# One product for both row halves in 28 weight-stationary units of a float32 transformer forward pass

## What is computed

```
def cross_attention(h, mem_n, wq, wkv, wo):            # layers 0 and 1
    q = (h @ wq).reshape(B, S, X_HEADS, X_HEAD_DIM)
    kv = (mem_n @ wkv).reshape(B, M, 2, X_HEADS, X_HEAD_DIM)
    s = einsum('bshd,bmhd->bhsm', q, kv[:, :, 0]) * X_HEAD_DIM ** -0.5      # 1/16
    ...
def odd_mixer(h, w_in, conv_w, w_out):                 # layer 1
    proj = h @ w_in                                    # b_gate, c_gate and a third part
    z = c_gate * proj[..., 2 * CONV_DIM:]
    ...
def sq_relu_mlp(h, w1, w2):                            # all three layers, width 4096
    a = relu(h @ w1)
    return (a * a) @ w2
c_act = silu(c)                                        # layer 2: mod = c_act @ w_ada + b_ada
```

## Time and profile before

| | |
|---|---|
| median of 3 runs | 1117.59 us (1115.75 to 1118.85) |
| the profiled execution | 1117.57 us, span 1115.7 us |
| TensorE busy | 1092.0 us (98%) in 6758 products |
| VectorE busy | 701.3 us (63%) |
| ScalarE busy | 517.7 us (46%) |
| weights and other data read | 222.95 MB, 201 GB/s over the span |
| granted TensorE clock | 0.998 of full speed |

### The profile page before, as it was taken

How to read it: one execution, slowest core, us unless ns; L and a number is a source line. 1 busy time by engine, 2 the same in 40 slices (tenths; PEclk the granted TensorE clock), 3 DMA queues, 4 the chain that set the end, 5 groups by cost and what they waited for, 6 DMA issues and landing times.

```text
span 1115.7 us, 15646 instructions
## 1 busy us (share of the span) xinstructions
PE 1092.0 (98%) x6758; PEld 978.5 (88%) x6758; DVE 701.3 (63%) x666; ACT 517.7 (46%) x584; POOL 65.0 (6%) x116
## 2 busy tenths in 40 slices
PE   6999999999999999999999999999999998999998
PEld 4989899898989989998988898997888877898997
DVE  4656565487577667666546757667767477555543
ACT  5555554354444445334445453444564464453441
POOL 2200000000000000000001000001201010000000
PEclk9999999999999999999999999999999999999999
DMA  9835454446775765554545767576335373655531
GB/s 360 323 142 170 159 200 157 165 171 246 262 289 190 294 245 208 183 189 153 213 140 210 271 258 286 198 279 236 120 135 173 140 245 114 226 189 189 189 114 38
DMA packets 32356, 225.05 MB, mean 202 GB/s; under 512 B 3748, under 2 KB 4064, under 8 KB 7584
## 3 DMA queue, kind: packets, MB, share of 16 engines
q1 hardware_dynamic: 26640, 188.03, 46.8%
q0 software_dynamic: 5120, 34.85, 8.8%
q10 hardware_dynamic: 528, 1.16, 0.3%
HBM read 222.95 MB, written 1.08 MB: 201 GB/s over the span
## 4 chain that ended last, share of the span: by engine, by line
PE 92%; DVE 5%; ACT 1%; issue 1%; POOL 1%; DMA 0%; DVEq 0%; ACTq 0%; POOLq 0%
PE ps L485 46%; PE ps L470 38%; DVE lo L1540 1%; PE ps L545 1%; PE ps L723 1%; PE ps L744 1%; ACT hi L1062 1%; PE ps L898 0%; DMA h<-in_x 0%; PE ps L944 0%; DVE lo L1536 0%; DVE h L1577 0%; PE ps L877 0%; PE ps L668 0%; DVE work L1931 0%
## 5 line engine op out<-in xcount | busy, mean ns | idle before, releaser
L1540 DVE TENSOR_TENSOR lo<-raw,hi 128x2048 fp32r<-128x2048 f32 x171 | 390.9, 2289 | 180.4 <-ACT hi L1062 180.2
L1062 ACT ACTIVATE hi<-raw 128x2048 fp32r<-128x2048 f32 x171 | 326.8, 1913 | 299.4 <-PE ps L485 160.1
L470 PE MATMUL ps<-xt_hi,hi 128*128 128x256 f32 x1088 | 308.8, 284 | 0.0
L470 PE MATMUL ps<-xt_hi,lo 128*128 128x256 f32 x1088 | 307.9, 283 | 0.0
L470 PE MATMUL ps<-xt_lo,hi 128*128 128x256 f32 x1088 | 307.9, 283 | 0.0
L485 PE MATMUL ps<-hi,yt_hi 128*128 128x512 f32 x544 | 213.1, 392 | 2.8 <-DVE yt_lo L1829 1.4
L485 PE MATMUL ps<-lo,yt_hi 128*128 128x512 f32 x544 | 211.8, 389 | 0.0
L485 PE MATMUL ps<-hi,yt_lo 128*128 128x512 f32 x544 | 211.8, 389 | 0.0
L470 PEld LDWEIGHTS ps<-xt_hi,lo 128*128 128x128 f32 x1088 | 208.8, 192 | 0.8 <-issue 0.2
L470 PEld LDWEIGHTS ps<-xt_hi,hi 128*128 128x128 f32 x1088 | 208.8, 192 | 0.8 <-issue 0.2
L470 PEld LDWEIGHTS ps<-xt_lo,hi 128*128 128x128 f32 x1088 | 208.8, 192 | 0.0
(11 more groups left out here) (261 smaller groups left out, 1048.7 us busy)
## 6 DMA issues: line engine op xcount, KB each, us to landing
raw<-in_weights SPq DMA_DIRECT2D x176, 1024.0 KB, 5.0
work<-in_w_ada POOLq DMA_DIRECT2D x16, 1536.0 KB, 7.3
work<-in_gains POOLq DMA_DIRECT2D x6, 512.0 KB, 4.2
work<-mod_rows POOLq DMA_DIRECT2D x6, 512.0 KB, 7.3
h<-in_x SPq DMA_DIRECT2D x2, 512.0 KB, 6.2
work<-in_gains ACTq DMA_DIRECT2D x2, 512.0 KB, 7.1
work<-in_mem POOLq DMA_DIRECT2D x2, 512.0 KB, 9.2
work<-in_pool SPq DMA_DIRECT2D x1, 1024.0 KB, 16.1
```

The source lines that it names most:

```text
L470: mm = pe.matmul(o, ws[:, slot, k, j * P:(j + 1) * P], xs[:, c, :], start=(c == 0 and n == 0 and j % 2 == 0), stop=(c == KC - 1 and n == 2 ...
L1062: act.activation(hi[:, p % RING], raw[:, p % RING], ACT.Copy).then_inc(hi_ready, 1)
L1540: dve.tensor_tensor(lo[:, p % RING], raw[:, p % RING], hi[:, p % RING].bitcast(F32), ALU.subtract)\
```

## The change

- `unit_m` takes the place of `unit_w` in 28 units: the four query units, the first unit of each half of the convolution, and 22 of the 24 first-weight units of the MLPs (the two done by tile stay). For each weight block it multiplies the upper weights with upper and lower rows in one product of 512 columns, and the lower weights with the upper rows in one of 256 columns. For this the upper and lower rows lie side by side in one tensor (`xt`, `mt`).
- Such a unit fills four banks. ScalarE copies the second halves (`low_parts`), VectorE adds the first halves to them (`sums`), and each bank is free after its sum.
- In the MLPs both units of a round use banks 4 to 7 (2, 3, 6, 7 in the round done by tile). VectorE does ReLU and square in one instruction, ScalarE rounds it to `yt_hi`.
- Both query units use banks 2, 3, 0, 1; the convolution's merged units too, its other units 4, 5 and 6, 7.
- The factor 1/16 of the queries moves from the evictions to the splits of their weights.
- `ada_columns` is done at eight named places of each MLP; none is left for after it.
- Silu is one instruction of ScalarE.

```diff
+        def unit_m(u, x, banks, waits=((), ()), hooks={}):
+            for b in range(2):
+                slot = POS[(u, b)] % RING
+                for j in range(4):
+                    if (b, j) in hooks:
+                        hooks[b, j]()
+                    if j == 0:
+                        need(u, b)
+                        wait_all(waits[b])
+                    if b == 0:
+                        claim(banks[j], ("u", u, j))
+                    o = ps[:, banks[j], :]
+                    for k in range(HC):
+                        c = b * HC + k
+                        js = slice(j * P, (j + 1) * P)
+                        pe.matmul(o, hi[:, slot, k, js], flat(x[2][:, c]), start=(c == 0), stop=False,
+                                  skip_group_check=True)
+                        mm = pe.matmul(o[:, 0:S], lo[:, slot, k, js], x[0][:, c, :], start=False,
+                                       stop=(c == KC - 1), skip_group_check=True)
+                    if b == 1 and j < 3:
+                        filled_by(mm, ("u", u, j))
+                used(mm, u, b, ("u", u, 3) if b else None)
...
-            unit_w(u, XT, (2, 3), split(x))
-            unit_w(u + 1, XT, (0, 1), hooks={(0, 2): both(scores, 0, 1)})
+            unit_m(u, XT, (2, 3, 0, 1), split(x))
+            unit_m(u + 1, XT, (2, 3, 0, 1), hooks={(0, 2): both(scores, 0, 1)})
...
-                    unit_w(u, XT, (4, 5))
-                    unit_w(u + 1, XT, (6, 7))
+                    unit_m(u, XT, range(4, 8))
+                    unit_m(u + 1, XT, range(4, 8))
...
+        def low_parts(u, dst):                                   # ScalarE
+            for n in range(2):
+                b0 = fills["u", u, 2 * n][0]
+                act.wait_ge(*fill(("u", u, 2 * n)))
+                act.wait_ge(*fill(("u", u, 2 * n + 1)))
+                act.activation(dst[:, 2 * n:2 * n + 2, :], ps[:, b0:b0 + 2, S:NB], ACT.Copy)\
+                    .then_inc(*low_kept.up((u, n)))
+        def keep_low(u, dst):
+            refill(u, 0)
+            low_parts(u, dst)
+            refill(u, 1)
...
+        def sums(u, dst):                                        # VectorE
+            for n in range(4):
+                label = ("u", u, n)
+                dve.wait_ge(*low_kept.at((u, n // 2)))
+                dve.tensor_tensor(dst[:, n, :], bank(label)[:, 0:S], dst[:, n, :], ALU.add).then_inc(*free(label))
...
+                    sums(u + c, cut(r, 4))
+                    for n in range(4):
+                        dve.wait_ge(*read(("u", u + c, n)))
+                    dve.scalar_tensor_tensor(r, r, 0.0, r, ALU.max, ALU.mult).then_inc(*hid_sq.up((m, j, c)))
+                    refill(u + c, 1)
                     dve.wait_ge(*hid_hi.at((m, j, c)))
...
-        act.activation(c_tmp, c_act, ACT.Exp, scale=-1.0).then_inc(*c_exp.up(0))
+        act.activation(c_act, c_act, ACT.Silu).then_inc(*c_ready.up(0))
```

More of the change, by code:

```diff
@@ L412, in turn_bank @@
         return 4 + 2 * (T - 1 - t) + j
+    MERGED = []
+    for _u in range(NU):
+        name = NAME[_u]
+        if (name in ("q0", "q1")
+                or (name == "conv" and (_u - UNIT["conv"]) % 3 == 0)
+                or (name in ("mlp0", "mlp1", "mlp2") and (_u - UNIT[name]) % 4 < 2
+                    and (int(name[3]), (_u - UNIT[name]) // 4, (_u - UNIT[name]) % 4) not in BY_TILE)):
+            MERGED.append(_u)
+    low_kept = signal("low_kept", [(u, n) for u in MERGED for n in range(2)])
+    ADA_AT = [(0, 1), (0, 2), (1, 0), (1, 1), (1, 2), (2, 1), (2, 2), (3, 1)]
+    QUERIES = [UNIT[n] + a for n in ("q0", "q1") for a in range(2)]
     block = ctx.enter_context(nc.Block())
@@ L817, in _ @@
         for n in range(6):
-            unit_w(UNIT["conv"] + n, XT, (2, 3) if n % 2 == 0 else (0, 1), split("mix1") if n == 0 else ((), ()),
-                   {(1, 0): mod_turn(0, 7)} if n == 3 else {})
+            if n % 3 == 0:
+                unit_m(UNIT["conv"] + n, XT, (2, 3, 0, 1), split("mix1") if n == 0 else ((), ()),
+                       {(1, 0): mod_turn(0, 7)} if n == 3 else {})
+            else:
+                unit_w(UNIT["conv"] + n, XT, (4, 5) if n % 3 == 1 else (6, 7))
         pair(UNIT["conv_out"], ((yt_ready.at(("conv", 0)),), (yt_ready.at(("conv", 1)),)))
@@ L1078, in copy0 @@
                 .then_inc(*free(("u", u, 0)))
+            refill(u, 1)
+        def low_parts(u, dst):
+            for n in range(2):
+                b0 = fills["u", u, 2 * n][0]
+                assert fills["u", u, 2 * n + 1][0] == b0 + 1
+                act.wait_ge(*fill(("u", u, 2 * n)))
[5 more added lines that the diff above has]
+            low_parts(u, dst)
             refill(u, 1)
@@ L1309, in mlp @@
                         continue
[L1310 to L1319, removed]
+                    keep_low(u + c, cut(hn[:, c, :], 4))
+                    act.wait_ge(*hid_sq.at((m, j, c)))
+                    act.activation(yt_hi[:, 4 * c:4 * c + 4, :], cut(hn[:, c, :], 4), ACT.Copy)\
+                        .then_inc(*hid_hi.up((m, j, c)))
                 if j < 3:
@@ L1342, in _ @@
                 act.wait_ge(*conv_z.at(0))
-            copy0(u, gate_c[:, 0:2, :])
+            keep_low(u, gate_c)
             if b == 1:
@@ L1847, in cross, with ada_columns @@
             refill(uo + 1, 0)
-        def ada_columns(m, i, a):
-            load = 8 * m + 2 * i + a
+        def ada_columns(load):
             dve.wait_ge(ada_landed, 16 * (load + 1))
@@ L1910, in _ @@
             u = UNIT["conv"] + 3 * b
-            copy1(u, gate_c[:, 2:4, :])
-            for n in range(2):
+            keep_sums(u, gate_c)
+            for n in range(4):
                 dve.wait_ge(*read(("u", u, n)))
```

64 lines of the change are left out of this document (34 added, 30 removed).

## The result

| | before | after |
|---|---|---|
| median | 1117.42 us (5 runs, 1115.75 to 1118.85) | 1110.35 us (5 runs, 1110.06 to 1111.86) |
| ratio to before | | 0.9943, 95% interval 0.9933 to 0.9954 |
| profiled execution | 1117.57 us, span 1115.7 us, clock 0.998 | 1111.86 us, span 1110.0 us, clock 0.998 |

The forecast was 1106.8 us with a range of 1104.0 to 1112.5: the sign and the range held, the size did not. So the medians differ by 7.1 us, but like executions by 5.7 to 5.9 us, and that is the change's worth: half of what was forecast.

A forecast was written before the change was run, and what follows sets the result against it. The prediction took TensorE's instruction stream, busy for 98% of the span, to bound the kernel. Its terms -11.6 + 0.1 + 1.0 - 0.35 = -10.8 us took 1117.57 us to 1106.8 us, range 1104.0 to 1112.5.

The forecast's parts named there:

- Part 1, the price of a group: Merged units on TensorE: three products become two, 359.8 to 346.9 ns a group, 896 groups, -11.6 us.
- Part 1, by tile: By-tile MLPs: transposes waiting for VectorE sit inside the merged unit, so four groups ahead give nothing back, +0.1 us.
- Part 2, banks: Successive merged units sharing four banks: the first add frees its bank 0.8 us before the claim, so no wait, 0.
- Rival (a): Shared banks: adds one weight split later make TensorE wait 1.5 us at 12 places, +18 us, 1124.8 us; chance 0.05.
- Part 2, the hidden layer: MLP: the second unit's parts are ready 6.3 or 7.4 us after it, needed at 10.9 us, so hidden.
- Part 2, cross-attention: Both cross-attentions: ScalarE's copy of the last two banks precedes its split, 0.5 us on each chain, +1.0 us.
- Part 3, the convolution: Convolution's output pair: its wait for a bank held by the third unit's product goes, -0.35 us.
- Part 3, `ada_columns`: Moving each MLP's last ada_columns ahead of the boundary takes 3.5 us of VectorE where TensorE does not wait: nothing.
- Part 4: The query factor in the weight splits and silu on ScalarE, with a possible covered table load: at nothing.
- (b): Merged products: the fixed part goes with column count or shape switching, so nothing is saved, 1118.3 us; chance 0.06.
- Rival (c): Part of the banks or of cross-attention waits, losing 3 to 6 us, 1110 to 1113 us; chance 0.08.
- (d): Merged products: the lower weights' load hides, the remaining two products lose the fixed part too, 35 us, 1083; chance 0.03.

The follow-up runs named there:

- three_products: The kernel after with each group of a merged unit as three 256-column products again, evictions and banks as changed: 1117.77 us.
- both_512: The kernel after with the lower weights multiplied with both row halves too, so all products of a merged unit have 512 columns: 1201.25 us, one execution.
- runs of two, four and eight: The kernel after issuing two, four or eight 512-column products, then as many 256-column ones (eight also with late cross-attention copy): 1106.0 (one), 1109.88, 1108.19 us.
- adds_late: The kernel after with VectorE doing the first weight split of a pair's first merged unit twice, at 10 MLP places, delaying the adds: 1127.59 us.
- cross_late_copy: The kernel after with the second query unit's copy and adds of its last two banks moved behind the weight split, in both cross-attentions: 1110.82 us.
- ada_back: The kernel after with the last ada_columns of MLP 0 and MLP 1 back behind the next layer's boundary: 1111.61 us.
- no_silu: The kernel after with silu back as ScalarE's exponential and VectorE's addition, reciprocal and product ahead of the first MLP: 1118.34 us.
- grouped: The kernel after with a merged unit's products in runs of four, four of 512 columns and then four of 256: 1109.88 us.
- two_banks: The kernel after in runs of two, but the two products of a run go to two banks instead of one: 1110.46 us, one execution.
- grouped2: The kernel after with a merged unit's products in runs of two, two of 512 columns and then two of 256: 1106.0 us, one execution.

## Why the prediction was right and where it was wrong

- **What bounds the kernel: right.** The gain came from TensorE's stream alone; three_products, which keeps the stream as it was, is as slow as before.
- **Part 1, the price of a group: wrong, and this is the failed step.** The prediction said that no row shows the mixed pattern, and then took that each kind keeps its own spacing, 12.9 ns saved a group. Measured were 359.8 - 353.3 = 6.5 ns: 5.9 us over 896 groups instead of 11.6. The ground given was that the one hand-over from a 256-column run to a 512-column run has no gap in the chain. That is so, but the products behind it are dear (233, 236, 228, 233 and 230 ns), which the timeline of before had and the chain's mean of 227 over 96 products hides. both_512 and the runs of two, four and eight show that the extra is bound to the mixture. The bounds of the term were 0 and 12.9 ns; it fell in the middle. The rule of the Trainium skill ("TensorE: Matmul & The Clock Gate", section "Back-to-back issue gap", N/2.4 + 2.5 ns), worth 2.5 ns a group, is off on the other side, and the starts at 236 and 117 ns fit it no better than those at 227 and 120; the page gives it for an isolated product, and not for a stream with weight loads as here.
- **Part 1, by tile: not separable.** 0.1 us is below what these traces tell.
- **Part 2, banks: right.** No wait of a merged line, and adds_late found the margin that the prediction worked out, 0.8 us. Rival (a)'s 1.5 us a place was right too.
- **Part 2, the hidden layer: right.** The pair starts at 304.54, with the unit's end, and runs 21.79 us without a wait; the second unit's lower parts are ready at 311.07, 6.5 us after the unit, where 6.3 or 7.4 were given (for the 7.4 no working is shown) and 10.9 allowed. The extra load on VectorE was put at some 40 us, though 28 x 1.7 is 48; measured are 25 us, with some 8.5 us of silu gone from it, and it cost TensorE nothing.
- **Part 2, cross-attention: right**, +1.0 us, taken back by cross_late_copy.
- **Part 3, the convolution: right.** The chain of after (answers to the earlier trace rows) has the pair at 473.55 + 23.04 = 496.59, at once, and the wait for the product with the third unit is gone from TensorE's waits:

```profile
473.55 23.04 PE ps L484 x192
496.58 3.43 PE ps L525 x15
```

- **Part 3, `ada_columns`: right** for the move behind the boundary, by ada_back.
- **Part 4: the cost right, the ground wrong.** Silu adds a table load of 1.28 us, and ScalarE still idles 1.66 us behind it:

```profile
176.52 1.28 ACT L1339 ACT_TABLE_LOAD   x1
179.46 0.47 ACT L1339 ACTIVATE hn<-ps,shift 128x256 f32<-128x256 f32 x1 [1.66 <-DVE shift L1889]
```

But "TensorE's weight-stationary line waited for nothing" was read as if the 8.5 us on VectorE had been free there in either kernel. They were free beside the old units; beside merged ones they cost 5.8 us, as no_silu shows. The step that was put at nothing is worth as much, beside merged units, as the whole change gains. A cover has to be looked up in the trace of the kernel as it will be, with the new deadlines, not in that of before.
- **The sum.** With the measured term it reads -5.9 + 0.1 + 1.0 - 0.35 = -5.15 us, and the profiled executions differ by 5.7. Some of the rest is that other rounds gain a little more: 44.82 - (1084.23 - 1039.84) = 0.43 us a round by the starts of the last two pairs in after's chain, 896/64 x 0.43 = 6.0. About 0.4 us is left with no row to it.
- **Rivals.** (b), nothing saved, had half a point: half of the fixed part was not the product's own in this order. Rival (c) named 1110 to 1113 us, where the time fell, but for waits that aren't there. So it was luck that the range held: its upper end of 1112.5 stood for (c) and for waits at the banks (whose own bounds, 1113 and 1106.8 + 6 = 1112.8, lie just above it), and the loss came from a term that the range did not open at all. (d) was wrong. None said that half of the fixed part might go; a term known to be between 0 and 12.9 ns with no row for the new pattern deserved a case of its own at the middle, 1117.57 - 5.8 + 0.75 = 1112.5 us.

## What to carry to other kernels

A cost that was measured in a stream of one shape is not the cost in a stream that mixes shapes: where the change makes a new mixture, price it between its bounds, look at the single starts behind a hand-over in the timeline and not only at the mean of a run, and try the order of the products, since here runs of two gave back four fifths of what runs of one lost. When a change makes two units share buffers, every long step in the queue of the engine that frees them gets a deadline; go through that queue at each place where the buffers are claimed. And where an ordering puts a copy ahead of the operation that heads the critical chain, move the copy behind it.

## What the runs showed that was not expected

**Mixed widths.** 128-row products of 512 and 256 columns, at 227 and 120 ns once they are among their own kind, come at 236 and 117 ns when they alternate, 233 and 115 in runs of two, about 232 and 118 in runs of four, 230 and 119 in runs of eight. The extra outlasts the hand-over: 512-column products settle at 227 ns only behind the fifth in before and in runs of eight, and behind the eighth in the pair that follows a merged unit in grouped (225 to 236 ns until then). That alone would make longer runs better; that runs of two beat them all does not follow from it. The runs show that the order sets this, and neither bank nor moving operand (two_banks), but not by what mechanism; that stays open.

**A fall of the clock at a boundary and behind a stall.** In the profiled executions the levels come from one place, the boundary of layer mix2, where TensorE works only in short pieces and idles up to 2 us between them. In after's profiled execution, chain and stretch:

```profile
775.31 1.95 issue
777.26 4.58 PE ps L525 x12
```

```profile
772.00:782.00 10.00, 7.51 (x30) 5.53 (x29) 8.44 (x11) 5.22 (x11) 3.72 (x9) 0.83 0.01 2
```

and in that of grouped2, the same twelve products and a stretch that holds them:

```profile
772.05 1.95 issue
774.00 2.97 PE ps L528 x12
```

```profile
772.00:782.00 10.00, 8.05 (x40) 6.66 (x40) 8.16 (x11) 8.63 (x12) 2.73 (x6) 1.00 0.14 42
```

Twelve products take 4.58 us in the one, in a stretch at a mean granted clock of 0.83, and 2.97 us in the other, at 1.00: 1.6 us, the distance of the levels. All eight executions profiled at 0.998 have this fall; of the four at 0.999 or 1.0 only both_512 has it. In adds_late, profiled at 0.996, it lasts longer: 0.57 from 787 to 795 us, the twelve products take 5.46 us, and that execution lies on a third level. The instructions and the idle time ahead of them are the same, so from one execution to the next it can go either way, which is why differences of 1 us had to be read between executions of one level. In no_silu the 4.3 us stall at 248.8 brought the same fall, 0.53, so a wait of 4.3 us cost 5.8.
